# A three-block forward pass on one core: neighbourhood attention three units deep, its gates copied out and their Silu batched, and a few other steps moved

## What is computed

```
s   = concat(q k_loc^T + bias (masked), q k_ctx^T)      # per row and head
p   = softmax(s)
o   = p v
out = concat(o, diff * subln_g, conv) * silu(gate)   @ w_out
```

## Time and profile before

| | us |
|---|---|
| median of 3 runs | 1847.93 |
| lowest and highest of them | 1841.69, 1852.33 |
| the profiled execution | 1851.54 |
| its span on the core | 1849.7 |
| PE busy | 1692.6 (92%) |
| DVE busy | 951.9 (51%) |
| ACT busy | 669.6 (36%) |
| POOL busy | 221.0 (12%) |
| mean granted TensorE clock | 0.944 of full |

### The profile page before, as it was taken

The page is one execution under the profiler, slowest core; times in us unless marked ns, Lnnn a source line. Parts: engine busy times, 40 slices in busy tenths (PEclk is TensorE's granted clock), DMA queues, the critical chain, the costliest instruction groups (busy, mean ns, idle before and its releaser), DMA issues.

```text
span 1849.7 us, 22824 instructions
## 1 busy us (share of the span) xinstructions
PE 1692.6 (92%) x8922; PEld 1319.2 (71%) x8922; DVE 951.9 (51%) x1662; ACT 669.6 (36%) x1249; POOL 221.0 (12%) x230
## 2 busy tenths in 40 slices
PE   7999977988999999979998899979989978987897
PEld 6866756876888888868887678845548866776553
DVE  1233263255656566465277766446654565563462
ACT  3254442333223323343215543334433245323341
POOL 3044223230000000121001100001110000000000
PEclk9998988999999999989999999979999989997699
DMA  7211042324564755333141120320012321221000
GB/s 261 69 35 58 23 182 85 103 73 115 166 173 103 171 146 141 126 114 109 42 147 41 52 69 1 118 98 1 12 44 87 120 74 52 69 91 69 1 12 35
DMA packets 170834, 161.34 MB, mean 87 GB/s; under 512 B 39958, under 2 KB 153864, under 8 KB 170696
## 3 DMA queue, kind: packets, MB, share of 16 engines
q1 hardware_dynamic: 167592, 150.04, 26.7%
q0 software_dynamic: 2848, 9.74, 1.4%
q10 hardware_dynamic: 288, 0.10, 0.0%
HBM read 149.80 MB, written 11.18 MB: 87 GB/s over the span
## 4 chain that ended last, share of the span: by engine, by line
PE 79%; DVE 12%; ACT 3%; issue 3%; DMA 1%; POOL 1%; ACTq 0%; SPq 0%; DVEq 0%; POOLq 0%
PE psum L2350 43%; PE psum L2321 12%; PE psum L2378 7%; PE psum L2808 6%; PE psum L2369 4%; PE psum L2479 2%; PE psum L2422 2%; DVE arena L1776 1%; DVE stat L2230 1%; PE psum L2403 1%; PE psum L2699 1%; DVE wring_r L1853 1%; DVE arena L1755 1%; DVE wring_r L1859 1%; DVE hT L1792 1%
## 5 line engine op out<-in xcount | busy, mean ns | idle before, releaser
L2350 PE MATMUL psum<-hT_r,wring_r 128*128 128x512 f32 (+1 forms) x1768 | 593.1, 394 | 0.0
L2350 PEld LDWEIGHTS psum<-hT_r,wring_r 128*128 128x128 f32 (+1 forms) x1768 | 330.8, 187 | 81.0 <-issue 8.6
L2350 PE MATMUL psum<-arena_r,wring_r 128*128 128x256 f32 (+2 forms) x1416 | 382.1, 337 | 1.8 <-DVE arena_r L1899 1.8
L1399 ACT ACTIVATE arena<-psum 128x512 f32<-128x512 f32 (+5 forms) x247 | 147.4, 620 | 504.3 <-PE psum L2350 289.2
L2321 PE MATMUL psum<-arena 128*128 128x96 f32 (+9 forms) x1460 | 240.0, 393 | 22.1 <-ACT arena L1399 11.3
L2350 PEld LDWEIGHTS psum<-arena_r,wring_r 128*128 128x128 f32 (+1 forms) x1416 | 229.0, 191 | 32.1 <-issue 4.2
L2321 PEld LDWEIGHTS psum<-arena 128*128 128x128 f32 (+5 forms) x1460 | 172.9, 205 | 85.7 <-issue 48.4
L2378 PE MATMUL psum<-ident,arena 128*128 128x128 f32 (+2 forms) x1028 | 145.4, 295 | 76.0 <-DVE arena L1755 42.7
L2350 PE MATMUL psum<-arena_r 128*128 128x512 f32 (+2 forms) x680 | 211.0, 351 | 0.0
L2378 PEld LDWEIGHTS psum<-ident,arena 128*128 128x128 f32 (+2 forms) x1028 | 126.1, 152 | 97.1 <-DVE arena L1755 47.1
L2350 PE MATMUL psum<-hT_r,arena_r 128*128 128x512 f32 (+1 forms) x408 | 163.7, 401 | 6.0 <-POOL wring_r L1303 6.0
(11 more groups left out here) (221 smaller groups left out, 2059.0 us busy)
## 6 DMA issues: line engine op xcount, KB each, us to landing
wring<-in_w_in_b SPq DMA_DIRECT2D x54, 512.0 KB, 5.9
arena<-in_w_mod SPq DMA_DIRECT2D x16, 1536.0 KB, 10.1
wring<-in_w_in SPq DMA_DIRECT2D x16, 1536.0 KB, 6.9
wring<-in_w_out SPq DMA_DIRECT2D x8, 2048.0 KB, 10.8
wring<-in_w_in_a SPq DMA_DIRECT2D x5, 1536.0 KB, 6.5
arena<-x_dram SPq DMA_DIRECT2D x3, 2048.0 KB, 13.4
wring<-in_w_in SPq DMA_DIRECT2D x6, 1024.0 KB, 5.5
arena<-ebias_dram SPq DMA_DIRECT2D x144, 32.0 KB, 1.8
```

The lines of the kernel that those rows point to most:

```text
L1399: return nc.scalar.activation(out, in_, ACT.Copy, scale=scale)
L2350: ins_ = nc.tensor.matmul(b[0:hi.shape[2], 0:width], w[:, k], v[:, k], start=k + p == 0, stop=(k, p) == (KT - 1, 2))
```

## The change

- **Units.** The depth is 3 in both layers (`DEPTH`). nS is only PE's now; M and E are steps of their own, nM and nE, two units ahead of nT, and nW(u+1) stands right behind nT(u). In C0 nPV(u-1) moves ahead of nT(u). The three pairs of probability buffers are shared; C0 has one buffer of transposed probabilities in place of two.
- **Gates.** Two gate steps stand ahead of the first unit, one behind each of nS(0) and nS(1), then one per unit. In C1 each gate is cut in two halves of 12 matmuls ("gatep" and "gate"). All of them use PSUM bank 7. They are copied out as they are, and Silu is applied in place afterwards, in batches (gS): features 0 to 2 once the third gate is there, features 3 to 7 (and in C0 the context's eight) after the first dF step. Scaling by `subw` becomes a step "subs" of each of the three dF k steps, ahead of their taps.
- **Taps.** 6, 6, 0 in place of 5, 5, 5 in the steps of nq in C0; one a unit in C1; the rest falls in the dF k steps.
- **Convolution and v.** cvT moves up from behind turn(2) to behind turn(0). dv and the last turn move behind the first dS, cvZ behind the second.
- **Block B.** The first call of `modulation()` goes, and one more stands in the last head, behind the gates. The rest of the splits of the first head's projections is computed by DVE in place of POOL.

The code that says so (cut; the splits' lookahead, buffers and semaphores that follow from it are left out):

```diff
@@ schedule
         add("aaavvvv", "BS", h)
-        modulation()
+        if h:
+            modulation()
...
             add("a", "gate", "B", 7)
+            modulation()
             add("avav", "BT", h)
...
             add(*keys[p])
+            if p == 0:
+                add("", "gS", l, 1)
+            add("", "subs", l, p)
             add("", "taps", l, ("k", p), 4 if both else 7)
...
         turn(0)
+        add("v" * (2 + both), "cvT", l)
         add(*queries[1])
...
-        for t in range(TT + CT):
-            add("av"[t % 2], "dv", l, t)
-        turn(6)
-        diff_stage(add, l)
+        def between():
+            for t in range(TT + CT):
+                add("av"[t % 2], "dv", l, t)
+            turn(6)
+        def then():
+            add("aa" * (1 + both), "cvZ", l)
+        diff_stage(add, l, between, then)
@@ neighbourhood
-    for u in range(depth):
-        add("aa", "nS", l, *units[u])
-        filled(fill[0][u])
+    filled(2)
+    for u in range(DEPTH):
+        add("aa", "nS", l, *units[u])
+        if u < 2:
+            softmax(u)
+            filled(1)
     add("", "nW", l, *units[0])
     for u, unit in enumerate(units):
+        if l == 0 and u:
+            product(u - 1)
         add("av", "nT", l, *unit)
-        if u:
-            n, j = units[u - 1]
-            add("v" * (j == NH // 2 - 1), "nPV", l, n, j)
-        filled(fill[1][u])
         if u + 1 < len(units):
             add("", "nW", l, *units[u + 1])
-        add("", "taps", l, ("n", u), 2 if l == 0 else fill[1][u])
-        if u + depth < len(units):
-            add("aa", "nS", l, *units[u + depth])
+        softmax(u + 2)
+        if l and u:
+            product(u - 1)
+        filled(1)
+        add("", "taps", l, ("n", u), 2 - l)
+        if u + DEPTH < len(units):
+            add("aa", "nS", l, *units[u + DEPTH])
@@ diff_stage
             add("aa", "dS", l, *items[n])
+        if n < 2:
+            (between, then)[n]()
@@ banks
-            free_ = (7,) if key[0] == "gate" and key[1] == "C1" else (4, 5, 7) if key[0] in ("gate", "gatec") and key[1] == "C0" else range(BANKS)
+            free_ = (7,) if key[0] in ("gate", "gatec") and key[1][0] == "C" else range(4, BANKS) if late(key) else range(BANKS)
@@ head_split
-            return n >= before_mem
+            return n >= split_at[("Bproj", 0, 0), 0]
@@ scalar
+                elif kind == "gate" and key[1][0] == "C":
+                    free(move(branch[:, key[2]], full(act, key, 0)[:, :]))
+                elif kind == "gS":
+                    l, part = key[1:]
+                    evacuated(act, ("gate", f"C{l}", (NH // 2, KT)[part] - 1))
+                    v = branch[:, part * NH // 2:KT if part else NH // 2]
+                    nc.scalar.activation(v, v, ACT.Silu).then_inc(gates_ready, 1)
+                    if part and l == 0:
+                        evacuated(act, ("gatec", "C0", KT - 1))
+                        nc.scalar.activation(cbranch, cbranch, ACT.Silu).then_inc(gates_ready, 1)
```

More of the change, by code:

```diff
@@ L37 @@
 HT_BANKS = 5
+DEPTH = 3
 MH, MD = 4, 64
@@ L271, in schedule @@
         turn(2)
-        add("v" * (2 + both), "cvT", l)
         add(*values[0])
@@ L275, in schedule @@
         add(*values[1])
-        add("aa" * (1 + both), "cvZ", l)
         turn(4)
@@ L301, in schedule @@
                 end -= 1
-            while split < min(n + units - (key[0] in ("Bproj", "BS") or key[0] == "hcT"), end):
+            while split < min(n + units - (key[0] in ("Bproj", "BS") or key[0] == "hcT") + (key[0] == "nq") - (key[:2] == ("gate", "C1")), end):
                 out.append((("split", split), ""))
@@ L389, in diff_items, with diff_stage @@
     return [(t, h) for t in diff_tiles(l) for h in range(DH)]
-def diff_stage(add, l):
+def diff_stage(add, l, between, then):
     tiles, items = diff_tiles(l), diff_items(l)
@@ L1542, in _ @@
                     free(nc.scalar.activation(dst, full(act, key, 0)[:, :], ACT.Silu))
-                elif kind == "gatec":
-                    free(nc.scalar.activation(cbranch[:, key[2]], full(act, key, 0)[:, 0:NMEM], ACT.Silu))
                 elif kind == "qm":
@@ L2198, in _ @@
                     l, n = key[1:3]
-                    for j in range(NH // 2):
-                        evacuated(dve, ("gate", f"C{l}", j))
+                    dve.wait_ge(gates_ready, gates_silu(l, 0, 0))
                     v = branch[:, 0:NH // 2].rearrange("p j (r n c) -> p n j r c", r=GRID_H, n=NQB)[:, n]
@@ L2333, in turn_tokens, with split_features @@
                 done(ins_)
-            def split_features(key, i, g, context):
+            def split_features(key, i, g, context, blocks=range(KT)):
                 n = split_at[("gate", *key[1:]) if key[0] == "gatec" else key, g]
@@ L2345, in split_features @@
                     evacuated(pe, ("hcT", key[1]), 3)
-                for k in range(KT):
+                for k in blocks:
                     if new and i == 0:
@@ L2426, in _ @@
                             turn_tokens(pe, ("hT", f"C{l}"), src, k + HT_BANKS)
+                elif kind == "gatep":
+                    split_features(("gate", *key[1:]), 0, 0, 0, range(KT // 2))
+                elif kind == "gate" and key[1] == "C1":
+                    split_features(key, 0, 0, 0, range(KT // 2, KT))
                 elif (split_jobs(key) and kind != "Aproj") or kind == "gatec":
```

117 lines of the change are left out of this document (66 added, 51 removed).

## The result

The change takes 1821.49 us (median of 4 runs, 1817.57 to 1824.54) against 1848.14 us for the kernel before in the same session: a ratio of 0.986, 95% interval 0.982 to 0.989. That is 26.6 us less, under half of the 55 us forecast, and inside the range. A second measurement of the same kernel gave 1818.85 us, 0.985 (0.983 to 0.987). The profiled execution spans 1820.6 us, 29.1 less than the 1849.7 before.

What follows compares the result with a forecast made beforehand. The prediction took PE as the bound, so only its waits and low clock behind them could go. Its terms summed to 55.5 us off the profiled 1851.5 us, 1796.0, or 1793 us as a median; range 1775 to 1824 us.

Steps and rivals of the forecast that it cites:

- units of C0: Neighbourhood stretch of C0: 21 us lost by waits and low clock, 2 us kept for what doesn't fit, 19 us gained.
- units of C1: Neighbourhood stretch of C1: 29.4 us lost by waits and low clock, 5.6 us of it stays, 23.8 us gained.
- cvT in C1: Convolution's transposes in C1: a 4.82 us wait and its slow clock, 6.8 us, go except 0.5 us; 6.3 us gained.
- dv and cvZ, C1: Start of C1's differential loop: transposes of v and cvZ moved into the waits for the exponentials, 3.3 us gained.
- dv, cvZ and the Silu batch, C0: C0's differential loop: moved transposes lose a net 1.4 us, the Silu batch behind the first dF step 0.5 us.
- modulation steps (and lo's), block B: Block B: 7.9 us at the first modulation step go, 3 us come back in the last head; lo's zero; 5 us gained.
- The 1 to 2 us of queue ahead of st_dram: Last head of block B: the new last chunk's 1.5 MB stand in the queue ahead of st_dram, costing 1 to 2 us.
- Bank 7: Rival "Slower", units of both stages: gates wait for ACT's copy to free their one bank, up to 1906 us; chance 0.04.
- the sign that the prediction itself had named for being wrong: Units: the forecast would be wrong if PE's waits named a gate's matmuls behind ACT (bank 7).
- 14.5 and 15 us fit: Units of C0: DVE's 14.5 to 15 us for two units fit PE's 15.0 us, with next to no room.
- Table loads: 28 of 61 loads of 1.28 us go; counted inside the units' 21 and 29 us, not as a separate gain.
- Half of it comes back: Rival, units of both stages: DVE takes 1 us more a unit and paces PE, 24 us less gain, 1817 us; chance 0.22.

Runs made afterwards that it cites:

- e1: The change with the modulation steps and the statistics' key on SP back where they stood before: 1814.8 us, ratio 0.982.
- e4: The kernel before with nothing but the move of the modulation steps and the statistics' key: 1851.9 us, ratio 1.001.
- e15: e11 with the change's order of the modulation steps: 1808.0 us, ratio 0.977.
- e8: The change with all transposes of v evicted by DVE: 1819.7 us, ratio 0.984.
- e11: The change with modulation steps and cvZ back, context gate's copy ahead of E, and all transposes of v evicted by DVE: 1798.5 us, ratio 0.973.
- e3: The change with ACT's copy of each context gate of C0 ahead of the unit's two exponentials: 1814.7 us, ratio 0.981.
- e12: The change with modulation steps, dv and cvZ back, context gate's copy ahead of E, and whole gates in C1: 1809.8 us, ratio 0.979.
- e9: The change with modulation steps, dv and cvZ back, context gate's copy ahead of E, and cvT back behind turn(2): 1808.5 us, ratio 0.978.
- e7: The change with each gate of C0 and C1 evicted as its Silu, as before: 1829.1 us, ratio 0.990.

## Why the forecast was wrong

The terms of the units held in kind and mostly in size. Two others came out with the opposite sign, and half of the gain was missing. By term, against the profiled execution (minus is faster):

| term | forecast | trace |
|---|---|---|
| units of C0 | -19.0 | -15.0 |
| units of C1 | -23.8 | -19.8 |
| cvT in C1 | -6.3 | -6.9 |
| dv and cvZ, C1 | -3.3 | +3.1 |
| dv, cvZ and the Silu batch, C0 | +1.9 | +4.7 |
| modulation steps (and lo's), block B | -5.0 | +4.6 |
| elsewhere | 0 | +0.2 |
| sum | -55.5 | -29.1 |

*Modulation, missed by 9.6 us: the step that failed.* "5 us gained" took the 7.9 us of head 0 as kept. They are there (PE is 8.1 us further ahead behind head 0), but the wait was a symptom of a queue: one slot for weights, each load issued only when the step before has been read, behind the statistics' way round and three split loads on SP. With PE 8 us ahead, five later steps wait 7.9 us, and at 673 us the two traces are level. In the last head "the new last chunk stands in head 5, where PE idles 6.3 us before the transposes anyway" was wrong about the place: it stands ahead of gates 6 and 7, not behind them, and so its own wait of 10.35 us fell on PE while 11 us of gate matmuls were ready behind it. I hadn't counted either that its 1.5 MB stand behind 4 MB of output weights. The 1 to 2 us of queue ahead of st_dram were right (the last read of the statistics is issued at 785.7 in place of 784.5 us). By 817 us the last head had lost 4.3 us in place of 3. e1, e4 and e15 show the whole term by itself; no run separates the last head from the queue before it, or has the product behind the gates.

*dv and cvZ behind dS, missed by 6.4 us in C1 and 2.8 in C0.* "Leave full stretches for this wait and the next" looked at PE's idle time and not at who evicts. Half of v's transposes are ACT's, behind the exponential that PE waits for; cvZ's Silu is behind the next one, and its bank is what the first transposes of probabilities claim. e8 and e11 show that with DVE evicting, v does fill the wait, and that cvZ doesn't belong there.

*Units of C0, missed by 4.0 us.* Bank 7 was named, as a rival, and its check was wrong: "PE claims the bank for the next gate after 7.0 us in C1 and 8.8 us in C0". 8.8 us holds behind a full gate. Behind a context gate PE claims it 1062.7 - 1056.5 = 6.2 us after the transposes' end, and the copy is through 7.6 us after it, because a lo and two taps stand ahead of M. 4.5 us of waits, shown by e3; it is the sign that the prediction itself had named for being wrong. Another 2.3 us stand at the stage's start: 1.5 us for DVE's eviction behind six taps, 0.8 us where the second gate step follows the first in the one bank. "14.5 and 15 us fit" was right: no transposes wait for W.

*Units of C1, missed by 4.0 us.* 6.4 us of waits and 1.7 us of low clock are left, 8.1 us where 5.6 were kept. The halves cost what I hadn't counted: 2.98 us each from start to start, 5.96 for the two against 5.67 for a whole gate, some 1.5 to 2.3 us over the stage's eight gates. e12 shows that whole gates give it back in waits.

*cvT.* The size was right, the reason was not borne out: the forecast put it on the place ahead of two turns; e9 shows that more taps between the units are enough.

*Table loads.* "They count inside the circle; in the sum they are part of the 21 and 29 us" was right in kind. e7 gives their share in the new order, 9 us. The Silu batch of C0 is in the 4.7 us of its row and isn't separated from dv and cvZ by any run.

*The rivals.* "Half of it comes back" forecast 1817 us and had the number nearly right, but not the cause: DVE doesn't pace the units. In the units 8 us came back, by bank 7 in C0 and by waits and the cut gates in C1; the rest did so in the stages to either side of them. That the number was near is luck.

The range, 1775 to 1824 us, held only because that rival was in it. e11, which has the modulation steps, cvZ and the context gate's copy changed, ends at 1798.5 us, 5.5 us above the forecast; it is another kernel and doesn't bear the forecast out.

## What to carry to other kernels

A wait of PE for a load is worth its length only if the next loads can come sooner as well; ask what each of them is issued behind before counting the gain. When a step is moved by shifting calls, look up in the list where its work now stands, and what ready work stands behind it. Work moved into a wait must be freed by an engine that isn't the one waited for, and its bank must not be the one that the waiting step claims next. A bank's circle has to be checked for the shortest piece of work between two claims, not for the average unit.

## What the runs showed of the hardware

- A table load isn't held by the wait of the instruction it is for. At 1066.35 us it ran during E's wait, so a switch ahead of a waiting instruction cost nothing. 32 more loads in the 24 units lost 9 us, not the 42 us that I had put down for two visible loads each.
- The same work of block B took 509.8 to 514.3 us in nine traces, and 511.8 to 521.6 us in nine with tighter loads; C0 and C1 repeat within 2.5 us. A few us of a schedule that leans on loads can't be told from one trace.
- A late landing can belong to one place of the program and not to chance. Of the sixteen loads of 1.5 MB for the modulation steps most land 6.8 to 13 us after their issue in all 18 traces. With the old order it is each time the tenth that is late, by 16.4 to 18.3 us (in the kernel before the one at 609.81 us, 16.5 us), and nothing waits for it; in e9 the eleventh takes 14.4 us as well. With the new order the tenth takes 12.6 to 15.7 us, and in the change its step waits 3.4 us, the longest of the five; the sixteenth takes 14.6 to 17.2 us, where with the old order it took 6.8 to 7.2. Why just these are late stays open.
